# Eight-core streaming encoder step: norm tiles turned by crossbar DMA instead of TensorE, two gate products per step, an earlier final norm

## The chip, the cores and the metric

The kernel runs on the 8 cores of one Trainium2 chip, the same program on each. A core has TensorE (PE) for matrix products and transposes, VectorE (DVE), ScalarE (ACT) and GpSimd (POOL) for the rest, SyncE (SP) for issuing DMAs, and 16 DMA engines. The metric is the device time of the slowest core in microseconds (us), the median of the runs.

## The reference

One layer of an encoder trunk over 4 x 8192 prompt tokens and 16 x 64 further tokens, width 1024. Cut to what matters here:

```python
h = _rmsnorm(x, norm1_g)
z = h @ w_in                                  # [pool a 512 | u 512 | v 512]
u, v = gelu(z[..., 512:1024]), gelu(z[..., 1024:])
pool_out = ((trailing_mean(a) - a) @ pool_w) * pool_scale
gmlp_out = u * (einsum('gij,bnjgd->bnigd', masked_ws, v) + gmlp_b)
x = x + concat([pool_out, gmlp_out]) @ w_out
f = _rmsnorm(x, norm2_g) @ w_up               # 1024 -> 4096
x = x + square(relu(f)) @ w_down              # 4096 -> 1024
y = _rmsnorm(x, normf_g)                      # the final norm
```

`_rmsnorm` scales each token (row) by the inverse root of its mean square and each column by `g`.

## The kernel before

Each core has 33 tiles of 128 tokens, in nine groups: group 0 has three tiles, group 1 two, groups 2 to 8 four each. x stays in `XS` (SBUF, nine slots of 128 tokens x 1024 channels, float32), weights come in blocks of 1 MB through the five slots of `RING`. TensorE contracts over the partition dimension, so a normalised tile (tokens on partitions) has to be turned: channels onto partitions, in eight 128-channel blocks.

A norm of tile n takes five parts. `N1_sq` or `N2_sq` (ACT, L316) sums the squares; `rs` (POOL, L323 and L324) makes the scale of two tiles; `N1_apply` or `N2_apply` (DVE, L330) writes the normalised bf16 tile into one of three `HB` buffers, in turn; `N1_T` or `N2_T` turns it: eight transposes on TensorE into a PSUM bank (L339) and a copy on ACT (L343) to `HT` for the first norm, `H2T` for the second. Both are one form of `norm_T`, with the tile's destination as an argument. `final_sq`, `final_rs` and `final_out` are the final norm; `final_out` also issues the store to `yall` from POOL's queue (L652), and `load_x` (L370) then loads a later group's tile into the slot that the store has left.

The order of each engine's work is written out by hand: a list `main` of steps for TensorE, and `side(k, ...)`, which hangs further work behind step k; `run` goes through both, and every helper appends to the queue of its engine (`add`). Engines run their own queues in order and wait on semaphores for what `reads` and `writes` name. A buffer that is still read makes its next writer wait.

The first two groups go through two passes together (`for c in range(2)`), which also make weight sums and differences in scratch memory; group 2's first half runs beside them. Then comes the loop over groups, `for i in range(2, NG)`: pass i does the MLP of group i and, as side work, the norms, input projection, mixers and output projection of group j = i + 1. Six passes, i = 2 to 7, have such a j; I count them from one ("the third pass" is i = 4). `main` of a pass has 60 steps: 32 up-projections `UP` (steps 0 to 31, L577; ACT's Relu, L582; VectorE's square, L584), then 28 down-projection parts `DN` (L624), seven products M of four steps each, in the order 3, 4, 5, 7, 2, 1, 6 (a fast form with seven in place of eight products). After the second half of a product VectorE adds its PSUM bank to x (L634); product 6 goes on in the bank of product 1, so step 56 needs the add behind step 54, and step 57 the one behind step 55.

The side work of group j by step: `load_x` at 6, `N1_sq` 17 to 20, `N1_apply` 21 to 24, `N1_T` 23 to 26, input projection `WI_au` 27 to 34 (L385, all of `HT` wanted) and `WI_v` 35 to 38 (L406), pool mixer `PL` 31 to 34, `gate` 39 to 42 (four small products, L475, then on VectorE an add, L482, and a product, L491), output projection `WO` 43 to 50 (L504; add to x, L509), `N2_sq` 48 to 51, `N2_apply` 53 to 56, `N2_T` 55 to 58. Step 0 of the next pass wants all of `H2T`. `UP` and `DN` use five PSUM banks in turn, all side work the other three (`next_front`).

Of the kernel before, what the change touches and what calls it, by code (L numbers as in the profile page):

```python
# [117 lines left out]
def build_nc():  # L118
# [35 lines left out]
    with contextlib.ExitStack() as es:  # L154
# [71 lines left out]
        def ht(i):  # L226
            return HT1 if i == 1 else HT[:, :, 16:528]
# [18 lines left out]
        def h2t(i):  # L246
            return H2T1 if i == 1 else H2T
# [11 lines left out]
        def schedule(P, order, record):  # L259
# [94 lines left out]
            def N1_T(i, n):  # L354
                hb = hbs[("1", i, n)]
                norm_T(HB[hb], [("HB", hb)], ht(i)[:, :, n * 128:(n + 1) * 128], ht_res(i, n))

            def N2_sq(i, n):
                sq("2", n, xap(i, n), [xres(i, n)])
# [403 lines left out]
            for c in range(2):  # L763
# [47 lines left out]
                else:  # L811
# [13 lines left out]
                    for n in range(4):  # L825
                        side(nup + 2 + n, L(N2_apply, 2, n))
                        side(nup + 4 + n, L(N2_T, 2, n))
                run(main, sides)

            for i in range(2, NG):  # L830
# [8 lines left out]
                            main.append(L(DN, i, M, c, n))  # L839
                prev = [(0, 0), (0, 1), (0, 2), (1, 0), (1, 1)] if i == 2 else [(i - 1, n) for n in range(4)]  # L840
                if i == 2:
                    side(0, *[L(final_sq, 0, n) for n in range(3)], L(final_rs, 0, 3))
                    side(2, *[L(final_out, 0, n) for n in range(3)])
                    side(3, *[L(final_sq, 1, n) for n in range(2)], L(final_rs, 0, 2))
                    side(5, *[L(final_out, 1, n) for n in range(2)])
                else:
                    side(0, L(final_sq, i - 1, 0), L(final_sq, i - 1, 1), L(final_rs, 0, 2))
                    side(1, L(final_sq, i - 1, 2), L(final_sq, i - 1, 3), L(final_rs, 2, 4))
                    for n in range(4):
                        side(2 + n // 2, L(final_out, i - 1, n))  # L850
# [6 lines left out]
                if j < NG:  # L857
                    for n in range(4):
                        side(6, L(load_x, j, n))
                        side(17 + n, L(N1_sq, j, n))  # L860
                        side(21 + n, L(N1_apply, j, n))
                        side(23 + n, L(N1_T, j, n))
                    side(18, L(rs, "1", 0, 2))
                    side(20, L(rs, "1", 2, 4))
                    for m in range(8):
                        side(27 + m, L(WI_au, j, m))
                    for n in range(4):
                        side(35 + n, L(WI_v, j, n))
                    side(31, L(PL_pre, j))
                    for g in range(4):  # L870
                        side(31 + g, L(PL, j, g))
                        side(39 + g, L(gate, j, g))
                    side(35, L(PL_post, j))
                    for hh in range(2):
                        for n in range(4):
                            side(43 + hh * 4 + n, L(WO, j, n, hh))
                    for n in range(4):
                        side(48 + n, L(N2_sq, j, n))
                        side(53 + n, L(N2_apply, j, n))
                        side(55 + n, L(N2_T, j, n))  # L880
                    side(49, L(rs, "2", 0, 2))
                    side(51, L(rs, "2", 2, 4))
                else:
                    side(55, L(final_sq, i, 0), L(final_sq, i, 1), L(final_rs, 0, 2))
                    side(56, L(final_out, i, 0, "sp"), L(final_out, i, 1, "sp"))
                    for n in (2, 3):
                        side(59, L(final_sq, i, n), L(final_rs, n, n + 1))
                    side(59, L(final_out, i, 2, "sp"), L(final_out, i, 3, "sp", 2))
# [77 lines left out]
```

How the kernel before makes its waits and increments, by code:

```python
        def run(engname, e, final=False):  # L77
            waited = {}
            pe_ch = prog.engchan["pe"]
            for fn, waits, chn in prog.ops[engname]:
                need = {}
                for w in waits:
                    if engname == "pe" and w.chan is pe_ch:
                        continue
                    if w.val > need.get(w.chan, 0):
                        need[w.chan] = w.val
                for ch, v in need.items():
                    if waited.get(ch, 0) >= v:
                        continue
                    e.wait_ge(ch.sem, v)
                    waited[ch] = v
                ins = fn(e)
                ins.then_inc(chn.sem, chn.inc)
            if final:
                for ev in final_waits:
                    e.wait_ge(ev.chan.sem, ev.val)
```

## Time and profile before

| | us |
|---|---|
| median of 3 runs (lowest, highest) | 1289.81 (1289.68, 1290.63) |
| the profiled execution | 1289.96 |
| its span on the slowest core (core 7) | 1288.2 |
| spans of the eight cores | 1284.0 to 1288.2 |
| TensorE busy | 1212.3 (94% of the span) |
| VectorE busy | 638.0 (50%) |
| ACT busy | 400.7 (31%) |
| DMA | 261.93 MB, mean 203 GB/s |
| transposes of norm tiles (L339) | 43.6 busy, 536 instructions |

The page gives busy time and shares for the whole span; the waits, the order of time and the DMAs come from queries of the trace, all of core 7. In the rows of the last section a timeline row has start, duration, engine, line, operation, what it writes and reads (`out<-in`), the shapes and the count of merged instructions; in brackets the idle time of its engine just before and what ended it. A waits row has the total, how often, and the longest. A DMA row has the count, the KB of each and the median time from issue to landing. A windows row has the busy time of PE, PEld (weight loads), DVE, ACT and POOL with the number of instructions, then TensorE's granted clock, the DMA engines' busy share and GB/s. Names such as `L339` are lines of the kernel; `ps` is PSUM.

### The profile page before, as it was taken

The numbers are of one execution on the slowest core, as the hardware profiler recorded it, in microseconds if no ns is written. First come the engines' busy times: TensorE is split into PE (matmuls) and PEld (weight loads), VectorE is DVE, ScalarE is ACT, GpSimd is POOL, SyncE is SP. The second block draws the span as 40 slices with busy tenths as digits, with TensorE's granted clock in tenths as the row PEclk, the third lists the DMA queues.
The fourth block names the chain that finished last, engine by engine and source line by source line (L and its number), as shares of the span: only waits on it lengthen the run. The fifth ranks groups of instructions, "written<-read, shape, count | busy, mean of one in ns | idle before, by whom it ended". The sixth has DMA issues, their size and how long they took to land.

```text
span 1288.2 us, 17796 instructions; the slowest of 8 cores (1284.0 to 1288.2 us)
## 1 busy us (share of the span) xinstructions
PE 1212.3 (94%) x6236; PEld 588.1 (46%) x6236; DVE 638.0 (50%) x1022; ACT 400.7 (31%) x678; POOL 100.8 (8%) x195
## 2 busy tenths in 40 slices
PE   5679998999799999999999999999999999999996
PEld 2336545543344444444444444444444444444442
DVE  2633636383355533665455534664455534764344
ACT  4324212314420255114520255114520355114301
POOL 4010000101000010001000010001000020001001
PEclk9879999999899999999999999999999999999998
DMA  9998866968634883457735783458634883758473
GB/s 179 187 228 227 183 198 203 163 225 280 196 120 174 262 270 122 163 198 279 243 119 175 261 283 114 173 193 282 230 131 164 270 278 110 186 200 281 175 262 145
DMA packets 44518, 261.93 MB, mean 203 GB/s; under 512 B 7360, under 2 KB 7488, under 8 KB 17552
## 3 DMA queue, kind: packets, MB, share of 16 engines
q1 hardware_dynamic: 31424, 206.84, 47.3%
q0 software_dynamic: 13008, 53.97, 18.3%
q8 instruction: 51, 0.84, 0.3%
q14 instruction: 35, 0.29, 0.1%
HBM read 240.22 MB, written 42.82 MB: 220 GB/s over the span
## 4 chain that ended last, share of the span: by engine, by line
PE 83%; DMA 6%; DVE 5%; issue 3%; ACT 1%; POOL 1%; DVEq 0%; POOLq 0%; SPq 0%; ACTq 0%
PE ps L577 25%; PE ps L624 25%; PE ps L504 9%; PE ps L385 8%; PE ps L538 5%; PE ps L552 5%; PE ps L406 4%; DMA XS<-xall 3%; PE ps L339 2%; DMA yall<-XS 2%; DVE HB L330 1%; DMA WSMT<-gmlp_ws 1%; DVE ps L482 1%; DVE XS L649 1%; ACT JUNK L316 1%
## 5 line engine op out<-in xcount | busy, mean ns | idle before, releaser
L577 PE MATMUL ps<-H2T,RING 128*128 128x512 bf16 x1792 | 399.3, 381 | 2.7 <-DMA RING<-scr_up 2.7
L577 PEld LDWEIGHTS ps<-H2T,RING 128*128 128x128 bf16 x1792 | 175.1, 98 | 210.9 <-issue 7.2
L624 PE MATMUL ps<-RING,ST 128*128 128x512 bf16 x1120 | 258.9, 379 | 0.0
L584 DVE TENSOR_TENSOR ST<-ST 128x512 bf16<-128x512 bf16 x224 | 93.8, 424 | 284.6 <-ACT ST L582 283.7
L582 ACT ACTIVATE ST<-ps 128x512 bf16<-128x512 f32 x224 | 132.2, 595 | 212.1 <-PE ps L577 210.4
L316 ACT ACTIVATE JUNK<-XS 128x1024 bf16<-128x1024 f32 x100 | 105.5, 1055 | 288.5 <-DVE XS L509 218.7
L634 DVE TENSOR_TENSOR XS<-XS,ps 128x512 f32<-128x512 f32 x140 | 96.1, 686 | 142.4 <-PE ps L624 138.0
L624 PEld LDWEIGHTS ps<-RING,ST 128*128 128x128 bf16 x1120 | 108.6, 98 | 126.5
L385 PE MATMUL ps<-HT,WAU 128*128 128x512 bf16 (+2 forms) x512 | 119.3, 379 | 0.6 <-ACT HT L343 0.6
L624 PE MATMUL ps<-RING,SB 128*128 128x512 bf16 x448 | 104.9, 379 | 0.0
L509 DVE TENSOR_TENSOR XS<-ps,XS 128x512 f32<-128x512 f32 x66 | 45.5, 689 | 68.4 <-PE ps L504 67.3
L385 PEld LDWEIGHTS ps<-HT,WAU 128*128 128x128 bf16 x512 | 50.9, 100 | 59.6 <-issue 3.6
L339 PE MATMUL ps<-IDB,HB 128*128 128x128 bf16 (+1 forms) x536 | 43.6, 228 | 36.1 <-DVE HB L330 35.1
L552 PE MATMUL ps<-RING,ST 128*128 128x512 bf16 x320 | 71.5, 379 | 0.0
L504 PE MATMUL ps<-RING,MIXP 128*128 128x512 bf16 x224 | 57.5, 379 | 8.1 <-DVE HT L491 8.1
L624 PEld LDWEIGHTS ps<-RING,SB 128*128 128x128 bf16 x448 | 42.8, 98 | 47.2
L406 PE MATMUL ps<-WV,HT 128*128 128x512 bf16 x248 | 59.6, 386 | 2.7 <-DMA WV<-w_v 2.7
L323 POOL TENSOR_SCALAR SS<-SS 128x2 f32<-128x2 f32 (+3 forms) x34 | 8.6, 253 | 671.4 <-ACT JUNK L316 671.2
L339 PEld LDWEIGHTS ps<-IDB,HB 128*128 128x128 bf16 (+1 forms) x536 | 36.6, 102 | 52.8 <-issue 41.6
L343 ACT ACTIVATE H2T<-ps 128x1024 bf16<-128x1024 bf16 x31 | 31.8, 1024 | 82.7 <-PE ps L339 82.7
L504 PE MATMUL ps<-RING,HT 128*128 128x512 bf16 x224 | 57.5, 379 | 0.0
L596 DVE TENSOR_TENSOR ST<-ST 128x1024 bf16<-128x1024 bf16 x84 | 54.9, 684 | 0.0
(84 smaller groups left out, 925.8 us busy)
## 6 DMA issues: line engine op xcount, KB each, us to landing
RING<-scr_dn SPq DMA_DIRECT2D x98, 1024.0 KB, 5.3
RING<-scr_up SPq DMA_DIRECT2D x56, 1024.0 KB, 7.6
RING<-w_mlp POOLq DMA_DIRECT2D x16, 1024.0 KB, 12.1
XS<-xall POOLq DMA_DIRECT2D x30, 512.0 KB, 16.3
yall<-XS POOLq DMA_DIRECT2D x29, 512.0 KB, 6.7
RING<-scr_wo SPq DMA_DIRECT2D x14, 1024.0 KB, 5.1
scr_dn<-RING SPq DMA_DIRECT2D x10, 1024.0 KB, 7.6
scr_up<-RING SPq DMA_DIRECT2D x8, 1024.0 KB, 9.5
```

What stands on the lines that cost most here:

```text
L316: add("act", lambda e: e.activation(out=JUNK[0:np_], in_=ap, func=AF.Square, scale=1.0 / 32, accum_out=SS[kind][0:np_, j:j + 1]), reads=re ...
L339: i_ = e.transpose(out=bankbf(fb)[:, k * 128:k * 128 + np_], in_=src[0:np_, k * 128:(k + 1) * 128], identity=IDB[0:np_, 0:np_])
L385: i_ = e.matmul(bank(fb)[:, 0:h0 + T], lhsT=WAU[:, m, k, :], rhs=rhs, start=(k == 0), stop=(k == 7))
L406: i_ = e.matmul(bank(fb)[:, :], lhsT=H[:, k, n * 128:(n + 1) * 128], rhs=WV[:, k, :], start=(k == 0), stop=(k == 7))
L504: i_ = e.matmul(bank(fb)[:, :], lhsT=mix(i, k, n * 128, (n + 1) * 128), rhs=W[:, k, :], start=(k == 0), stop=(k == 7))
L538: i_ = e.matmul(bank(ub)[:, 0:T], lhsT=RING[s][:, k, mm_ * 128:(mm_ + 1) * 128], rhs=HX[:, k, 0:T], start=(k == 0), stop=(k == 7))
L552: i_ = e.matmul(bank(ub)[:, :], lhsT=HID[h](j0 + kk, n * 128, (n + 1) * 128), rhs=RING[s][:, kk, :], start=(kk == 0), stop=(kk == 7))
L577: i_ = e.matmul(bank(ub)[:, :], lhsT=RING[s][:, k, (m % 4) * 128:(m % 4 + 1) * 128], rhs=H2T[:, k, :], start=(k == 0), stop=(k == 7))
L582: add("act", lambda e: e.activation(out=ST[:, m, :], in_=bank(ub)[:, :], func=AF.Relu), writes=[("BANK", ub)] + rr)
L584: add("dve", lambda e: e.tensor_tensor(out=ST[:, m, :], in0=ST[:, m, :], in1=ST[:, m, :], op=ALU.mult), writes=rr)
L624: i_ = e.matmul(bank(ub)[:, :], lhsT=lh(kk), rhs=RING[s][:, kk, :], start=(c == 0 and kk == 0 and M not in CONT), stop=(c == 1 and kk == 7 ...
L634: add("dve", lambda e, x=x, op_=op_: e.tensor_tensor(out=x, in0=x, in1=bank(ub)[:, :], op=op_), writes=[("BANK", ub), xres(i, rb * 2 + n)])
```

## The change

For groups 3 to 8, `N1_T` and `N2_T` are replaced by `N1_D` and `N2_D`: one DMA, issued by ACT, that reads the `HB` tile and writes it turned to `HT` or `H2T`. Groups 0 to 2 keep the transposes on TensorE. The squares and normalisations of both norms come earlier by some steps, the turned tiles too. The four gate products hang two by two behind steps 39 and 40. Group 0's final norm moves from the loop's first pass into the pass before it, and group 1's moves up behind steps 0 and 2. In the diff the new helpers come first, then the second pass of the first two groups (c = 1), the loop's first pass (i = 2), and the side work of group j.

```diff
+            def turn(src, res, dst, dst_res, nm):
+                add("act", lambda e: e.dma_start_transpose(out=dst, in_=src), reads=res, writes=dst_res, dma=nm)
+
+            def N1_D(i, n):
+                hb = hbs[("1", i, n)]
+                turn(HB[hb][:], [("HB", hb)], ht(i)[:, :, n * 128:(n + 1) * 128], ht_res(i, n), f"xb1_{n}")
+
+            def N2_D(i, n):
+                hb = hbs[("2", i, n)]
+                turn(HB[hb][:], [("HB", hb)], h2t(i)[:, :, n * 128:(n + 1) * 128], h2_res(i, n), f"xb2_{n}")
...
+                    for n in range(3):
+                        side(nup + 16 + n, L(final_sq, 0, n))
+                    side(nup + 18, L(final_rs, 0, 3))
+                    for n in range(3):
+                        side(nup + 19, L(final_out, 0, n))
...
-                    side(0, *[L(final_sq, 0, n) for n in range(3)], L(final_rs, 0, 3))
-                    side(2, *[L(final_out, 0, n) for n in range(3)])
-                    side(3, *[L(final_sq, 1, n) for n in range(2)], L(final_rs, 0, 2))
-                    side(5, *[L(final_out, 1, n) for n in range(2)])
+                    side(0, *[L(final_sq, 1, n) for n in range(2)], L(final_rs, 0, 2))
+                    side(2, *[L(final_out, 1, n) for n in range(2)])
...
-                        side(17 + n, L(N1_sq, j, n))
-                        side(21 + n, L(N1_apply, j, n))
-                        side(23 + n, L(N1_T, j, n))
-                    side(18, L(rs, "1", 0, 2))
-                    side(20, L(rs, "1", 2, 4))
+                        side(15 + n, L(N1_sq, j, n))
+                        side(18 + n, L(N1_apply, j, n))
+                        side(20 + n, L(N1_D, j, n))
+                    side(16, L(rs, "1", 0, 2))
+                    side(18, L(rs, "1", 2, 4))
...
-                        side(39 + g, L(gate, j, g))
+                        side(39 + g // 2, L(gate, j, g))
...
-                        side(48 + n, L(N2_sq, j, n))
-                        side(53 + n, L(N2_apply, j, n))
-                        side(55 + n, L(N2_T, j, n))
-                    side(49, L(rs, "2", 0, 2))
-                    side(51, L(rs, "2", 2, 4))
+                        side(47 + n, L(N2_sq, j, n))
+                        side(50 + n // 2, L(N2_apply, j, n))
+                        side(51 + n, L(N2_D, j, n))
+                    side(48, L(rs, "2", 0, 2))
+                    side(50, L(rs, "2", 2, 4))
```

The changed kernel has eleven lines more ahead of the loops, so its line numbers are higher by 11 from L366 on (L624 becomes L635, L475 becomes L486).

TensorE's queue around the gates, before (L624 is a step, L475 a gate product, L504 the output projection):

```order
L624 MATMUL ps<-RING,ST 128x512 x8
L475 MATMUL ps<-WSMT,V 128x128 x4
L624 MATMUL ps<-RING,SB 128x512 x8
L475 MATMUL ps<-WSMT,V 128x128 x4
L624 MATMUL ps<-RING,SB 128x512 x8
L475 MATMUL ps<-WSMT,V 128x128 x4
L624 MATMUL ps<-RING,SB 128x512 x8
L475 MATMUL ps<-WSMT,V 128x128 x4
L624 MATMUL ps<-RING,SB 128x512 x8
L504 MATMUL ps<-RING,MIXP 128x512 x4
```

The same place in the changed kernel (L635, L486, L515):

```order
L635 MATMUL ps<-RING,ST 128x512 x8
L486 MATMUL ps<-WSMT,V 128x128 x8
L635 MATMUL ps<-RING,SB 128x512 x8
L486 MATMUL ps<-WSMT,V 128x128 x8
L635 MATMUL ps<-RING,SB 128x512 x24
L515 MATMUL ps<-RING,MIXP 128x512 x4
```

Two gate products stand together now, and three steps lie between the last of them and the output projection in place of one.

VectorE's queue at the second norm, before, with the numbers of the `HB` buffers (L634 adds a down-projection bank to x, L509 the output projection, L330 normalises):

```order
L509 TENSOR_TENSOR XS<-ps,XS 128x512
L634 TENSOR_TENSOR XS<-XS,ps 128x512 x2
L330 SCALAR_TENSOR_TENSOR HB1<-XS,RS2,G2B 128x1024
L634 TENSOR_TENSOR XS<-XS,ps 128x512
L330 SCALAR_TENSOR_TENSOR HB2<-XS,RS2,G2B 128x1024
L634 TENSOR_TENSOR XS<-XS,ps 128x512
L330 SCALAR_TENSOR_TENSOR HB0<-XS,RS2,G2B 128x1024
L330 SCALAR_TENSOR_TENSOR HB1<-XS,RS2,G2B 128x1024
L634 TENSOR_TENSOR XS<-XS,ps 128x512 x2
```

The same place in the changed kernel (L645, L520):

```order
L520 TENSOR_TENSOR XS<-ps,XS 128x512
L330 SCALAR_TENSOR_TENSOR HB1<-XS,RS2,G2B 128x1024
L330 SCALAR_TENSOR_TENSOR HB2<-XS,RS2,G2B 128x1024
L645 TENSOR_TENSOR XS<-XS,ps 128x512 x2
L330 SCALAR_TENSOR_TENSOR HB0<-XS,RS2,G2B 128x1024
L330 SCALAR_TENSOR_TENSOR HB1<-XS,RS2,G2B 128x1024
L645 TENSOR_TENSOR XS<-XS,ps 128x512 x4
```

All four normalisations stand ahead of the last four adds now, and the fourth writes the buffer (`HB1`) that the first turn reads.

ACT's queue there, before (L397 and L411 take the input projection out of PSUM, L316 is a square, L582 the next pass's first Relu):

```order
L582 ACTIVATE ST<-ps 128x512
L397 ACTIVATE UT<-ps 128x512 x4
L411 ACTIVATE V<-ps 128x512 x4
L316 ACTIVATE JUNK,SS<-XS 128x1024 x4
L343 ACTIVATE H2T<-ps 128x8x128 x4
L582 ACTIVATE ST<-ps 128x512
```

And in the changed kernel (L593, L408, L422):

```order
L593 ACTIVATE ST<-ps 128x512
L408 ACTIVATE UT<-ps 128x512 x4
L422 ACTIVATE V<-ps 128x512 x4
L316 ACTIVATE JUNK,SS<-XS 128x1024 x4
L359 DMA_TRANSPOSE H2T<-HB 128x8x128 x4
L593 ACTIVATE ST<-ps 128x512
```

Where ACT copied four turned tiles out of PSUM it now issues four DMAs that turn them, all of them behind the fourth square. In the first norm each of the four stands behind one Relu, as the copies did.

## Rows read from the trace of the kernel before

**Rows 1.** The page, parts 1 and 4: busy time (share), instructions; chain's shares.
```profile
PE 1212.3 (94%) x6236; PEld 588.1 (46%) x6236; DVE 638.0 (50%) x1022; ACT 400.7 (31%) x678; POOL 100.8 (8%) x195
...
PE 83%; DMA 6%; DVE 5%; issue 3%; ACT 1%; POOL 1%; DVEq 0%; POOLq 0%; SPq 0%; ACTq 0%
```

**Rows 2.** Waits of TensorE (us, times, longest): whole span, then 300 to 1171.
```profile
PE ps L339 <- DVE HB L330: 35.1, 15, 13.6
...
PE ps L339 <- DVE HB L330: 9.3, 3, 7.4
PE ps L504 <- DVE HT L491: 8.1, 6, 1.6
PE ps L577 <- DMA RING<-scr_up: 2.7, 1, 2.7
```

**Rows 3.** Timeline of TensorE, third pass: start, us, instruction [idle before].
```profile
595.04 41.60 PE L577 MATMUL ps<-H2T,RING 128*128 128x512 bf16 x192
...
730.41 0.61 PE L339 MATMUL ps<-IDB,HB 128*128 128x128 bf16 x8
730.86 1.89 PE L624 MATMUL ps<-RING,ST 128*128 128x512 bf16 x8
...
739.10 21.10 PE L577 MATMUL ps<-H2T,RING 128*128 128x512 bf16 x97
```

**Rows 4.** Timeline around the fourth gate product, third pass: VectorE, TensorE.
```profile
694.93 0.69 DVE L491 TENSOR_TENSOR HT<-ps,UT 128x512 bf16<-128x512 f32 x1
...
695.88 1.02 PE L504 MATMUL ps<-RING,MIXP 128*128 128x512 bf16 x4 [1.30 <-DVE HT L491]
```

**Rows 5.** Timeline of ACT and VectorE at that pass's second norm.
```profile
722.89 1.06 ACT L316 ACTIVATE JUNK<-XS 128x1024 bf16<-128x1024 f32 x1 [2.25 <-DVE XS L509]
...
725.17 1.28 DVE L330 SCALAR_TENSOR_TENSOR HB<-XS,RS,G2B 128x1024 bf16<-128x1024 f32 x1
```

**Rows 6.** Timeline of the loop's first pass: TensorE, ACT, POOL.
```profile
307.60 29.47 PE L577 MATMUL ps<-H2T,RING 128*128 128x512 bf16 x128 [2.72 <-DMA RING<-scr_up]
344.52 1.01 PE L339 MATMUL ps<-IDB,HB 128*128 128x128 bf16 x8 [7.45 <-DVE HB L330]
...
341.02 1.06 ACT L316 ACTIVATE JUNK<-XS 128x1024 bf16<-128x1024 f32 x1 [2.83 <-DMA XS<-xall]
...
300.56 0.62 POOL L652 DMA_DIRECT2D yall<-XS  x1 [2.12 <-DVE XS L649]
...
324.61 0.53 POOL L370 DMA_DIRECT2D XS<-xall  x1 [2.05 <-DMA yall<-XS]
```

**Rows 7.** Third pass: POOL's last x load; DMA issues (median us to landing).
```profile
616.79 0.53 POOL L370 DMA_DIRECT2D XS<-xall  x1 [4.55 <-DMA yall<-XS]
...
XS<-xall POOLq DMA_DIRECT2D x4, 512.0 KB, 14.4
```

**Rows 8.** DMA issues in 1265-1288, 1090-1105, 629-646, 718-740; SP's timeline.
```profile
yall<-XS SPq DMA_DIRECT2D x2, 256.0 KB, 2.2
...
RING<-scr_dn SPq DMA_DIRECT2D x2, 1024.0 KB, 10.4
...
spp<-A SPq DMA_DIRECT2D x1, 30.0 KB, 10.7
...
RING<-scr_dn SPq DMA_DIRECT2D x3, 1024.0 KB, 4.8
...
RING<-scr_up SPq DMA_DIRECT2D x5, 1024.0 KB, 7.8
RING<-scr_dn SPq DMA_DIRECT2D x1, 1024.0 KB, 6.2
...
722.03 0.32 SPq L296 DMA_DIRECT2D RING<-scr_dn  x1
```

**Rows 9.** Windows: engines' busy us (instructions), granted clock, DMA share, GB/s.
```profile
629.00:646.00 17.00, 17.00 (x104) 8.68 (x103) 9.73 (x15) 11.82 (x19) 1.87 (x4) 1.00 0.39 145
...
724.00:739.00 15.00, 15.00 (x95) 7.80 (x94) 7.90 (x9) 4.14 (x5) 0.93 (x2) 1.00 0.96 310
```

## The prediction

> **What bounds the kernel now.** I read the busy shares first, then who waited for whom on TensorE, then single passes in order of time, then the DMAs. TensorE is busy 94% of the span and the chain that ended last runs through it for 83% [rows 1]. It waits 35.1 us for normalised rows before their transposes, but only 9.3 of that in the loop over groups, beside 8.1 for the gate and 2.7 for a weight block [rows 2]; the other 25.8 us lie ahead of the loop, where the change leaves the norms as they are. Of the 9.3, 7.4 fall in the loop's first pass [rows 6], the rest, 1.9, in two later ones. In a pass of that loop TensorE has no gap but 1.3 us ahead of the output projection [rows 4]: what leaves its queue there comes off the time, as long as nothing new is late. One step of such a pass, eight products, is 41.60 / 24 = 1.73 us, and one pass is 144.1 us, 595.04 to 739.10 [rows 3]; the granted clock there is 1.00, the 2.4 GHz level [rows 9], and fewer gaps give it no cause to fall. The profiled execution took 1289.96 us, 1.8 over its span and 0.15 over the median, so I count from 1289.96.
>
> **Transposes (removed).** A turn of one norm tile, eight 128x128 transposes, moves the next product from 730.41 to 730.86 [rows 3]: 0.45 us of TensorE's queue, not the 0.61 its row shows, since ends overlap. Six passes hold eight turns each, 48 in all: 48 x 0.445 = **-21.4 us**. ACT loses 48 copies out of PSUM; it is 31% busy [rows 1], so that is worth nothing by itself.
>
> **Gates (moved).** The four gate products stood behind steps 39 to 42; the last is multiplied by VectorE at 694.93 to 695.62, and the projection starts at 695.88 after 1.30 us of waiting [rows 4]. Two per step starts the last product two steps (3.5 us) earlier, and VectorE has nothing between the eight gate operations now: the wait goes, six times, 8.1 us [rows 2]. The fourth product takes the PSUM bank of the first and so waits for its two VectorE operations, 1.4 us after it was made, against one step of 1.73 us, with one add ahead of them in VectorE's queue; I put 0.15 us on each pass. Sum **-7.2 us**.
>
> **First group's final norm (moved).** In the first pass the last x tile of the next group is asked for at 324.61, behind an output store, its square starts at 341.02 after waiting for it, and TensorE stands 7.45 us until 344.52 [rows 6]. The change sends the first group's stores out in the pass before, by its place about 7 us ahead of 300.56 [rows 6], the second group's with them, and the loads behind both on POOL's queue. With the square also two steps earlier, the last tile is then ready about when step 27 wants it. Counting the 1.9 us of later passes, -9.3 us, of which I give 1 back. The other side: the three early stores, 1.5 MB, meet the up-projection loads that already cost 2.72 us at 307.60 [rows 6], in a stretch where DMA is not idle. Between nothing (the wait even goes, -2.7) and 8 us I take +3, since 512 KB at the 310 GB/s of a busy stretch [rows 9] is 1.7 us. Sum **-5.3 us**.
>
> **Crossbar turns (added).** No row shows one, so its time L from issue on ACT's queue to landing has to be bounded. Low end: a plain 256 KB store in the quiet end of the program lands in 2.2 us. High end: 30 KB in 512 small pieces took 10.7 us [rows 8]. Where does L begin to cost?
> Second norm: ACT's fourth square ends near 724.0 [rows 5], and all four turns stand behind it. There are three HB buffers, so the fourth normalisation on VectorE waits for the first turn to land: 724.0 + L, plus 1.28 [rows 5]. Behind it in VectorE's queue stands the add that empties the bank of step 54, 0.69 us like the gate's operation, and step 56, at 730.41 [rows 3], accumulates into that bank: TensorE waits once L is over 4.4 us. The fourth turn lands at 725.3 + 2L; the next pass's first product, due 737.3 without the transposes (730.41 plus four steps of 1.73), waits once L is over 6.0.
> First norm: the last x tile is asked for at 616.79 and lands 14.4 us later [rows 7], 631.2; the square, two more Relus, and ACT reaches the first turn near 633.6. The fourth normalisation waits for it here too, so the fourth turn lands at 634.9 + 2L, and the input projection of step 27 wants it at 595.04 + 28 x 1.73 = 643.5: TensorE waits once L is over 4.3. This stretch is quiet, DMA 0.39 busy; the second norm's is not, 0.96 [rows 9].
> I take 4 us in the quiet stretch and 5 in the busy one: nearest is the 256 KB transfer, the same bytes, at 2.2; weight loads of 1 MB go from 4.8 to 7.8 us between the two stretches [rows 8], which makes it 3.6 in the busy one, and the rest is a surcharge for small pieces. So the first norm costs nothing and the second 0.6 us. The turns also lengthen the weight loads beside them: the block asked for at 722.03 lands after 6.2 us at 728.2 [rows 8], 2.2 us before step 56 wants it; I put another 0.6 us there. 6 x 1.2 = **+7 us**, between 0 and, at L = 7.8 throughout, 6 x (7.0 + 3.6) = 64.
> The Trainium skill, page "DMA: Bandwidth & Descriptors", section "Latency and other measured facts", gives DMA transposes 261 GB/s; the 256 KB of a turn would then move in 1.0 us (an estimate from that page), L would stay below both limits, and the sum would be 1256. No run here shows it yet.
>
> **Sum.** 1289.96 - 21.4 - 7.2 - 5.3 + 7 = **1263 us**. With every turn and load hidden it is 1289.96 - 21.4 - 8.1 - 9.3 - 2.7 = 1248.
>
> **Rivals.**
> (a) Slower: the crossbar works in small pieces, and a turn takes the 10.7 us of the small-piece row. Then the first norm's fourth turn is 634.9 + 21.4 - 643.5 = 12.8 us late and the second's 725.3 + 21.4 - 737.3 = 9.4 us: 22.2 us in each of six passes, 133 us against a gain of 34, near 1389. It decides from L = 6.6 on, where 4L - 20.6 eats the 5.65 us that a pass gains. For it: the small-piece transfers also stretched the 1 MB load beside them to 10.4 us [rows 8]. Against it: those pieces are 60 bytes and go to HBM. The Trainium skill, page "VectorE: DVE Perf Modes", section "The three transpose paths", speaks for it: 1309 ns for a 128x128 block by DMA against 390 ns on TensorE. Eight blocks one after the other would be 10.5 us (an estimate from that page), much as in (a), near 1384; its TensorE figure does not hold here, where a block costs 0.445 / 8 = 56 ns of queue.
> (b) L lies between: 6.6 to 7.8 us, 1291 to 1320.
> (c) The turns land in time, but the weights don't. From step 52 on TensorE uses up 1 MB per two steps, 3.45 us, and DMA already moves 310 GB/s at 0.96 share [rows 9]. Four turns bring 1 MB more, read and written: 3.4 to 6.8 us of transfer. The block of step 56 has 2.2 us in hand, the first up block, asked for one step (1.73 us) after that one and 7.8 us under way, is there at 731.6 and wanted at 737.3: 5.7 us. So 1 to 4.6 us come back as TensorE waits for RING; at 2.7 a pass it is 1279.
> (d) The change doesn't do what it says: the transposes' time is not free. Against it stands that the four steps with a turn each take 739.10 - 730.41 = 8.69 us, 2.17 apiece, where others take 1.73 [rows 3]. Only a chance balance of gain and wait would give 1290.
>
> **How the numbers follow.** The forecast (1248 to 1271) has 0.50, (c) 0.17, no change 0.04, (b) 0.11, (a) 0.18. A measurement of this kernel can tell about 0.2%, 2.6 us, from no change. Faster is the forecast and (c): 0.67; slower is (a) and (b): 0.29. The range reaches from everything hidden, 1248, to the upper end of (b), 1320, and holds 0.82; the likeliest case's own range is 1248 to 1271.
>
> **What would show it.** Right: 384 fewer transposes on TensorE; passes some 140.5 us apart instead of 144.1; no wait ahead of the output projection; ACT's turns landing in 3 to 5 us. Steps wrong one by one: a wait of the up-projection for H2T, or of the input projection for HT, says L is over its limit; a wait of the down-projection for XS's adds says VectorE stood at its fourth normalisation; waits for RING say (c); a wait longer than 2.72 us near 300 us says the early stores cost more than they bring. The prediction fails as a whole if L is over 6.6 us.

## The result, and the profile after

The changed kernel took **1486.5 us** (median of 4 runs, 1472.53 to 1501.62); the kernel before took 1289.87 beside it (4 runs). The ratio is 1.1431, 95% interval 1.1407 to 1.1456: 14% slower. The prediction said 1263, with a range of 1248 to 1320. It was wrong in size and in sign. Medians here and below are of all runs of a kernel and ratios of its undisturbed runs alone (here 1472.53 and 1476.37), so the two can differ; for first_norm_only and second_norm_only, which have no ratio, the profiled run is taken.

The profiled execution took 1472.53 us, its span on core 6 is 1471.0; the spans of the other cores reach from 1402.3 to 1470.1. First the page, parts 1 and 4, which answer to [rows 1]: busy time (share) and instructions, then the chain that ended last, by engine and by line.

```profile
PE 1214.8 (83%) x5747; PEld 571.5 (39%) x5852; DVE 636.2 (43%) x1022; ACT 354.2 (24%) x630; POOL 108.5 (7%) x195
...
PE 65%; DMA 18%; ACTq 8%; DVE 3%; issue 3%; ACT 2%; POOL 1%; DVEq 0%; SPq 0%; POOLq 0%
PE ps L588 23%; PE ps L635 15%; DMA H2T<-HB 10%; ACTq L359 8%; PE ps L515 8%; PE ps L396 7%; PE ps L549 4%; PE ps L417 4%; DMA HT<-HB 4%; PE ps L563 3%; DMA XS<-xall 2%; DMA scr_dn<-RING 2%; DVE HB L330 1%; ACT JUNK L316 1%; DMA RING<-scr_up 1%
```

TensorE went from 94% to 83% busy. 22% of the chain (10 + 8 + 4) is now the turns: two tiles of DMA and ACT's queue while it issues them (L359). The waits of TensorE over the whole span answer to [rows 2] (us, times, longest; L588 is the up-projection, L635 the down-projection, L645 its add to x, L396 the input projection):

```profile
PE ps L588 <- DMA H2T<-HB: 123.3, 6, 27.6
PE ps L635 <- DVE XS L645: 51.8, 6, 13.0
PE ps L339 <- DVE HB L330: 24.2, 12, 13.3
PE ps L396 <- DMA HT<-HB: 11.0, 5, 7.3
PE ps L588 <- DMA RING<-scr_up: 5.5, 1, 5.5
```

Three waits are new: 123.3 for the second norm's turned tiles, 51.8 for the adds behind VectorE's fourth normalisation, 11.0 for the first norm's tiles. The gate's 8.1 us is gone. The DMA issues of the whole span (count, KB, median us from issue to landing) show the price of a turn:

```profile
RING<-scr_up SPq DMA_DIRECT2D x56, 1024.0 KB, 11.4
...
HT<-HB ACTq DMA_TRANSPOSE x24, 4.4
H2T<-HB ACTq DMA_TRANSPOSE x24, 27.3
```

A first-norm turn lands in 4.4 us, a second-norm turn in 27.3. Core 6 is the slowest core; on the other seven the medians are 4.6 to 6.8 and 19.6 to 23.6. The up blocks take 11.4, where the same row of the kernel before has 7.6:

```profile
RING<-scr_up SPq DMA_DIRECT2D x56, 1024.0 KB, 7.6
```

**One second norm in order of time.** In the loop's second pass on core 6, the timelines of SP, ACT, VectorE and TensorE read:

```profile
614.08 66.34 SPq L296 DMA_DIRECT2D RING<-scr_up  x8
...
614.39 30.85 ACTq L359 DMA_TRANSPOSE H2T<-HB  x4
...
627.83 1.28 DVE L330 SCALAR_TENSOR_TENSOR HB<-XS,RS,G2B 128x1024 bf16<-128x1024 f32 x1 [9.78 <-DMA H2T<-HB]
629.03 1.28 DVE L645 TENSOR_TENSOR XS<-XS,ps 128x512 f32<-128x512 f32 x2
...
629.97 9.05 PE L635 MATMUL ps<-RING,ST 128*128 128x512 bf16 x31 [9.06 <-DVE XS L645]
657.03 50.61 PE L588 MATMUL ps<-H2T,RING 128*128 128x512 bf16 x220 [18.01 <-DMA H2T<-HB]
```

SP begins to send the next pass's up blocks at 614.08 and ACT the turns at 614.39. ACT needs 30.85 us only to issue the four. The first turn has landed when VectorE's fourth normalisation starts, 627.83: 13.4 us after its issue began. The other three, asked for one by one, landed 30.8, 28.9 and 22.4 us after their issue. The add runs at 629.03, TensorE has stood 9.06 us for it, and later stands 18.01 us for the fourth turn. Windows of the same stretch (length; busy time and instructions of PE, PEld, DVE, ACT, POOL; granted clock, DMA share, GB/s) show what the waits left behind:

```profile
596.00:614.00 18.00, 17.95 (x84) 8.15 (x84) 11.92 (x19) 4.23 (x7) 0.93 (x2) 1.00 0.64 222
614.00:630.00 16.00, 6.88 (x32) 2.98 (x32) 6.11 (x8) 0.37 (x2) 1.73 (x2) 0.81 1.44 184
630.00:633.00 3.00, 3.00 (x8) 1.05 (x9) 0.30 (x1) 0.00 (x0) 0.00 (x0) 0.50 0.30 75
630.00:657.00 27.00, 8.97 (x31) 3.45 (x32) 1.68 (x3) 0.00 (x0) 0.00 (x0) 0.69 0.90 152
657.00:660.00 3.00, 2.97 (x8) 1.07 (x9) 0.00 (x0) 0.00 (x0) 0.00 (x0) 0.50 0.16 68
657.00:675.00 18.00, 17.92 (x73) 7.79 (x75) 7.83 (x12) 8.88 (x17) 5.52 (x11) 0.88 0.45 161
```

Before the turns 84 products took 17.95 us at clock 1.00 (2.4 GHz), 0.214 each. The first 3 us behind TensorE's 9 and 18 us of standing have a granted clock of 0.50, the 1.2 GHz level. From 630 to 657, the 18 us of standing included, it averages 0.69, from 657 to 675 it averages 0.88, and 31 products take 8.97 (0.289 each), 73 take 17.92 (0.245 each). That is 31 x 0.075 + 73 x 0.032 = 4.7 us more in this pass.

The DMA engines look full from 630 to 657, share 0.90, yet move 152 GB/s. The queues in 612 to 660 (packets, MB, share of 16 engines; q10 is ACT's queue with the turns, q1 SP's) and the issues:

```profile
q10 hardware_dynamic: 4224, 1.05, 54.0%
q1 hardware_dynamic: 864, 6.29, 46.8%
...
RING<-scr_up SPq DMA_DIRECT2D x5, 1024.0 KB, 21.3
...
H2T<-HB ACTq DMA_TRANSPOSE x4, 25.6
```

Four turns are 4224 packets, 1056 apiece, of 1.05 MB / 4224 = 250 bytes. Their times add up to 0.54 x 48 x 16 = 415 us, 98 ns a packet. A share over 1, as the 1.44 from 614 to 630, means that times of packets overlap, so this is how long a packet was under way, waiting included, and not how long it kept an engine from others. The five up blocks beside them land in 21.3 us.

**Where the time went.** The span grew by 1471.0 - 1288.2 = 182.8 us. The new waits are 123.3 + 51.8 + 11.0 = 186.1; the waits for RING grew by 5.5 - 2.7 = 2.8. The gains: 21.4 of transposes, 8.1 at the gate, 35.1 - 24.2 = 10.9 for normalised rows. Together +148.5. Of the 34 us left, the slower clock after the waits makes up most if the pass above is typical: 6 x 4.7 = 28.

### The profile page after: what moved, and what is told of

It is laid out like the page before. It is cut to its first block, busy times and chain, and to the rows that moved or that the text cites. A ratio compares the mean times of both kernels' runs of the same rounds, so it can differ in the third digit from the quotient of the medians.

```text
span 1471.0 us, 17011 instructions; the slowest of 8 cores (1402.3 to 1471.0 us)
## 1 busy us (share of the span) xinstructions
PE 1214.8 (83%) x5747; PEld 571.5 (39%) x5852; DVE 636.2 (43%) x1022; ACT 354.2 (24%) x630; POOL 108.5 (7%) x195
## 3 DMA queue, kind: packets, MB, share of 16 engines
q10 hardware_dynamic: 50688, 12.59, 13.4%
## 4 chain that ended last, share of the span: by engine, by line
PE 65%; DMA 18%; ACTq 8%; DVE 3%; issue 3%; ACT 2%; POOL 1%; DVEq 0%; SPq 0%; POOLq 0%
PE ps L588 23%; PE ps L635 15%; DMA H2T<-HB 10%; ACTq L359 8%; PE ps L515 8%; PE ps L396 7%; PE ps L549 4%; PE ps L417 4%; DMA HT<-HB 4%; PE ps L563 3%; DMA XS<-xall 2%; DMA scr_dn<-RING 2%; DVE HB L330 1%; ACT JUNK L316 1%; DMA RING<-scr_up 1%
## 5 line engine op out<-in xcount | busy, mean ns | idle before, releaser
L588 PE MATMUL ps<-H2T,RING 128*128 128x512 bf16 x1756 | 407.6, 391 | 130.9 <-DMA H2T<-HB 123.3
L588 PEld LDWEIGHTS ps<-H2T,RING 128*128 128x128 bf16 x1792 | 179.0, 100 | 355.7 <-issue 156.3
L635 PE MATMUL ps<-RING,ST 128*128 128x512 bf16 x1099 | 267.5, 393 | 52.9 <-DVE XS L645 51.8
L593 ACT ACTIVATE ST<-ps 128x512 bf16<-128x512 f32 x224 | 132.8, 596 | 502.2 <-PE ps L588 480.7
L635 PEld LDWEIGHTS ps<-RING,ST 128*128 128x128 bf16 x1120 | 112.2, 101 | 195.3 <-issue 71.9
L316 ACT ACTIVATE JUNK<-XS 128x1024 bf16<-128x1024 f32 x100 | 105.3, 1053 | 286.0 <-DVE XS L520 212.2
L645 DVE TENSOR_TENSOR XS<-XS,ps 128x512 f32<-128x512 f32 x140 | 95.4, 686 | 141.5 <-PE ps L635 136.8
L396 PE MATMUL ps<-HT,WAU 128*128 128x512 bf16 (+2 forms) x505 | 119.8, 382 | 12.1 <-DMA HT<-HB 11.0
L635 PE MATMUL ps<-RING,SB 128*128 128x512 bf16 x432 | 101.2, 379 | 0.8
L396 PEld LDWEIGHTS ps<-HT,WAU 128*128 128x128 bf16 x512 | 50.6, 100 | 72.8 <-issue 18.8
L520 DVE TENSOR_TENSOR XS<-ps,XS 128x512 f32<-128x512 f32 x66 | 45.5, 689 | 66.7 <-PE ps L515 65.6
L563 PE MATMUL ps<-RING,ST 128*128 128x512 bf16 x312 | 70.8, 379 | 0.4
L330 DVE SCALAR_TENSOR_TENSOR HB<-XS,RS,G2B 128x1024 bf16<-128x1024 f32 x33 | 41.6, 1279 | 56.4 <-DMA H2T<-HB 56.1
L323 POOL TENSOR_SCALAR SS<-SS 128x2 f32<-128x2 f32 (+3 forms) x34 | 15.5, 455 | 683.7 <-ACT JUNK L316 683.5
L635 PEld LDWEIGHTS ps<-RING,SB 128*128 128x128 bf16 x448 | 43.4, 98 | 50.0
L515 PE MATMUL ps<-RING,MIXP 128*128 128x512 bf16 x220 | 56.9, 379 | 1.5 <-DVE ST L555 1.3
L515 PE MATMUL ps<-RING,HT 128*128 128x512 bf16 x222 | 57.2, 379 | 0.1
L549 PE MATMUL ps<-H2T,RING 128*128 128x384 bf16 x256 | 48.5, 338 | 1.4 <-ACT H2T L343 1.4
L330 DVE SCALAR_TENSOR_TENSOR HB<-XS,RS,G1B 128x1024 bf16<-128x1024 f32 x33 | 42.0, 1280 | 16.0 <-DMA G1B<-norm_g 7.6
## 6 DMA issues: line engine op xcount, KB each, us to landing
RING<-scr_up SPq DMA_DIRECT2D x56, 1024.0 KB, 11.4
RING<-w_mlp POOLq DMA_DIRECT2D x16, 1024.0 KB, 12.8
```

The lines of the kernel that those rows point to most:

```text
L316: add("act", lambda e: e.activation(out=JUNK[0:np_], in_=ap, func=AF.Square, scale=1.0 / 32, accum_out=SS[kind][0:np_, j:j + 1]), reads=re ...
L330: add("dve", lambda e: e.scalar_tensor_tensor(out=HB[hb][:], in0=xap(i, n), scalar=RS[kind][:, n:n + 1], in1=gb[:], op0=ALU.mult, op1=ALU. ...
L396: i_ = e.matmul(bank(fb)[:, 0:h0 + T], lhsT=WAU[:, m, k, :], rhs=rhs, start=(k == 0), stop=(k == 7))
L515: i_ = e.matmul(bank(fb)[:, :], lhsT=mix(i, k, n * 128, (n + 1) * 128), rhs=W[:, k, :], start=(k == 0), stop=(k == 7))
L549: i_ = e.matmul(bank(ub)[:, 0:T], lhsT=RING[s][:, k, mm_ * 128:(mm_ + 1) * 128], rhs=HX[:, k, 0:T], start=(k == 0), stop=(k == 7))
L563: i_ = e.matmul(bank(ub)[:, :], lhsT=HID[h](j0 + kk, n * 128, (n + 1) * 128), rhs=RING[s][:, kk, :], start=(kk == 0), stop=(kk == 7))
```

## The experiments

In the expectations, A is the theory that the weight blocks beside the turns make them slow, C a rival that needs no such neighbours. In the later runs P looks for the cause in small pieces that share the DMA engines with the blocks, X in the turning itself, F in an early final norm that brings nothing. The recorded texts say what each expects. Ratios are to the kernel before on the same chip. Line numbers shift a little between kernels.

**no_turns.** Both norms go back to TensorE at their old steps; gates and early final norm stay.

```diff
-                        side(20 + n, L(N1_D, j, n))
+                        side(23 + n, L(N1_T, j, n))
...
-                        side(51 + n, L(N2_D, j, n))
+                        side(55 + n, L(N2_T, j, n))
```

> The changed kernel with both norms of groups 3 to 8 turned on TensorE again, at the steps of the kernel before; gates and the earlier final norm stay. Theory A (the crossbar turns are the whole loss, the two other parts gain what the prediction gave them, 7 and 5 us): 1270 to 1280 us, no TensorE wait ahead of the output projection, the 7.4 us wait of the loop's first pass gone. Theory B (a part of the loss comes from the moved gates or the early stores): over 1290 us.

Measured: 1283.35 against 1295.11, ratio 0.9914 (0.9895 to 0.9933), which is 11.1 us (8.6 to 13.5) of 1289.96. Without the turns, and the earlier steps that come with them, the change is a gain, so they alone make the loss. TensorE's waits from 300 to 1171:

```profile
PE ps L588 <- DMA RING<-scr_up: 6.0, 1, 6.0
PE ps L339 <- DVE HB L330: 5.2, 2, 4.2
```

The gate's 8.1 us is gone. The wait for normalised rows fell from 9.3 [rows 2] to 5.2, the one for an up block rose from 2.7 to 6.0.

**gates_only.** The two-by-two gates alone, everything else as before.

```diff
-                        side(39 + g, L(gate, j, g))
+                        side(39 + g // 2, L(gate, j, g))
```

> The kernel before with one part of the change alone: the four gate products two by two. Both norms are turned on TensorE at their old steps, and the first group's final norm stands at its old place. Theory A (each term of the prediction apart from the turns holds): the waits of the output projection for VectorE, 8.1 us in six passes, go, and 0.9 us of gate products waiting for a PSUM bank come in, so 0.9944 of the time before, 1282.6 on the chip of the profile of before. Theory F (the early final norm brings nothing, and the whole gain of 0.86% of the run without turns is the gates'): 0.991.

Measured: ratio 0.9943 (0.993 to 0.9955) in 5 rounds, 7.4 us (5.8 to 9.0). This is theory A's number, 0.9944, and F's 0.991 lies outside the interval; the gates are settled. What no_turns gained beyond that, 11.1 - 7.4 = 3.7 us, is left for the early final norm, with some 3 us of uncertainty.

**second_norm_only and first_norm_only.** One norm by DMA, the other on TensorE; the rest as in the changed kernel.

```diff
-                        side(20 + n, L(N1_D, j, n))
+                        side(23 + n, L(N1_T, j, n))
```

> The changed kernel with only the second norm of groups 3 to 8 turned by DMA; the first norm is turned on TensorE at the steps of the kernel before. Theory A: 1460 to 1500 us, the turns landing in 10 to 35 us as in the changed kernel. Theory B: about half the loss, near 1385 us.

Measured: the profiled run took 1463.45 against 1295.11, 13% slower; a second run took 1485.48. One norm carries all but a little of the loss, as A said. The turns landed in 27.0 us, as A had it too. TensorE's waits, whole span:

```profile
PE ps L588 <- DMA H2T<-HB: 94.0, 6, 23.1
PE ps L635 <- DVE XS L645: 71.4, 6, 15.6
```

The other kernel undoes the second norm's turns in the same way.

> The changed kernel with only the first norm of groups 3 to 8 turned by DMA; the second norm is turned on TensorE at the steps of the kernel before. Theory A (the loss is the second norm's turns, which run beside the next pass's weight loads): 1265 to 1280 us, the turns landing in 3 to 8 us, about 11 us of TensorE waits for HT. Theory B (crossbar traffic slows the kernel wherever it runs): well over 1300 us, landing times of 10 us and more here too.

Measured: the profiled run took 1313.24 against 1295.11, 1.4% slower; A had said a gain and some 11 us of waits, which was a miss. The wait and the turns' landing time:

```profile
PE ps L396 <- DMA HT<-HB: 31.0, 6, 7.3
...
HT<-HB ACTq DMA_TRANSPOSE x24, 5.9
```

At 5.9 us the turns are past the limit of 4.3 that the prediction worked out, and TensorE waits 31.0 / 6 = 5.2 us a pass. On the eight cores the turns' medians are 5.5 to 6.5, much as in the changed kernel (4.4 to 6.8). That the first norm's stretch isn't quiet for the whole of its turns is tested by first_norm_hold below.

**hold_weights.** The next pass's first up blocks are sent only after the second norm's turns have landed.

```diff
+                if key[0] == "up" and key[1] < 2 and key[-1] >= 3 and at not in st.setdefault("freed", set()):
+                    st.setdefault("held", []).append(at)
+                    return
...
+                    held = [("H2T", n) for n in range(4)] if (src[0] == "up" and src[1] < 4 and key[-1] >= 3) else []
...
+                if n == 3:
+                    for at in st.pop("held", []):
+                        st.setdefault("freed", set()).add(at)
+                        ring_load(at)
```

> The changed kernel, but the first up-projection weight blocks of the next pass are loaded only when the second norm's four turns have landed, so that only one or two down-projection blocks run beside them. Theory A (the turns are slow because their 256-byte packets share each DMA engine with 8 KB weight packets): the turns land in 3 to 8 us and TensorE waits under 10 us a pass for H2T, now partly for RING; 1300 to 1380 us. Theory C (four turns behind one another are slow by themselves, in ACT's queue or in the crossbar): landing times stay at 20 to 30 us and the weights come after them; 1480 us or more.

Measured: 1334.42, ratio 1.031 (1.0285 to 1.0335). TensorE's waits over the whole span, then the issues:

```profile
PE ps L404 <- DMA HT<-HB: 37.5, 6, 8.3
...
PE ps L596 <- DMA RING<-scr_up: 21.3, 8, 9.7
...
HT<-HB ACTq DMA_TRANSPOSE x24, 6.1
H2T<-HB ACTq DMA_TRANSPOSE x24, 3.3
```

This decides for A and against C: the same turns land in 3.3 us instead of 27.3 when no up blocks move beside them, and no row of TensorE's waits names a DMA to `H2T` any more. The price has moved: the held blocks come late (21.3 us for RING), and the first norm, untouched here, is over its limit (6.1 us, 37.5 of waits).

**plain_pieces and plain_rows.** The second norm's four DMAs stay where they are but copy instead of turning (the second norm's tile is left unturned): once in pieces of 256 bytes, once in rows of 2 KB.

```diff
-                turn(HB[hb][:], [("HB", hb)], h2t(i)[:, :, n * 128:(n + 1) * 128], h2_res(i, n), f"xb2_{n}")
+                add("act", lambda e: e.dma_start(out=h2t(i)[:, :, n * 128:(n + 1) * 128], in_=HB[hb][:].rearrange("p (k t) -> p k t", t=128)),
+                    reads=[("HB", hb)], writes=h2_res(i, n), dma=f"xb2_{n}")
...
+                add("act", lambda e: e.dma_start(out=H2T[:, 2 * n:2 * n + 2, :].rearrange("p k t -> p (k t)"), in_=HB[hb][:]),
```

> The changed kernel with the second norm's four DMAs as plain copies in place of turns: the same 256 KB from HB to H2T in pieces of 256 bytes, from ACT's queue with the same waits. The tile is not turned, so what the second half of the layer computes for groups 3 to 8 is left out of the comparison. Theory P (small packets beside 8 KB weight packets are what is slow): landing 10 to 30 us as with the turns, 1450 us or more. Theory X (the crossbar itself suffers from other traffic on the 16 engines, plain pieces don't): landing under 8 us, TensorE waiting under 3 us a pass for H2T, 1290 to 1320 us.

Measured: 1350.37 (quickest run 1347.16), ratio 1.0432 (1.041 to 1.0454). Waits of TensorE, then issues:

```profile
PE ps L636 <- DVE XS L646: 42.9, 6, 11.2
PE ps L397 <- DMA HT<-HB: 28.9, 6, 8.4
...
RING<-scr_up SPq DMA_DIRECT2D x56, 1024.0 KB, 7.9
H2T<-HB ACTq DMA_DIRECT2D x24, 256.0 KB, 12.2
```

> As the plain copy in 256-byte pieces, but each token's 2 KB goes to one place of H2T in one piece (not turned, so what the second half of the layer computes for groups 3 to 8 is left out of the comparison). Theory P: packets eight times as large, landing 3 to 6 us, 1290 to 1310 us. Theory X: the same. Together with the pieces it tells whether the bytes alone cost anything.

Measured: 1342.92 (1336.81 and 1349.03), ratio 1.0387 (1.033 to 1.0444).

```profile
PE ps L397 <- DMA HT<-HB: 35.6, 6, 8.6
PE ps L636 <- DVE XS L646: 25.9, 6, 5.5
...
H2T<-HB ACTq DMA_DIRECT2D x24, 256.0 KB, 8.2
```

So 256 KB beside the up blocks cost 8.2 us in long rows, 12.2 in 256-byte pieces, 27.3 turned. Neither P nor X has it alone: small pieces add 4 us, the turning another 15, and only the turning slows the blocks beside it (11.4 against 7.9). Only with the turning does TensorE wait for a DMA to `H2T`; neither copy leaves such a row. P had the landing of the pieces right and their time 100 us too high; for the rows both theories expected 3 to 6 us and at most 1310, a miss. Even the long rows miss the limit of 4.4 us for VectorE. A good part of what both copies lose is the first norm, which is still turned by DMA here (28.9 and 35.6).

**sp_queue.** All turns are issued by SP, in the queue of the up blocks.

```diff
-                add("act", lambda e: e.dma_start_transpose(out=dst, in_=src), reads=res, writes=dst_res, dma=nm)
+                add("sp", lambda e: e.dma_start_transpose(out=dst, in_=src), reads=res, writes=dst_res, dma=nm)
```

> The changed kernel with all turns issued from SP's queue, which also issues the weight loads, in place of ACT's. Theory P (a turn's packets take turns with the other queue's 8 KB packets): in one queue they only wait for what was issued before them, landing 3 to 10 us, no long wait for H2T, 1300 to 1390 us. Theory X: weight packets on the same engines still hold the crossbar up, landing 10 to 30 us, over 1430 us.

Measured: 1338.6, ratio 1.0353 (1.0332 to 1.0374).

```profile
PE ps L396 <- DMA HT<-HB: 30.6, 6, 7.1
PE ps L635 <- DVE XS L645: 29.9, 6, 5.7
...
H2T<-HB SPq DMA_TRANSPOSE x24, 7.7
```

In the blocks' own queue a turn of the second norm lands in 7.7 us, not 27.3. It is still over 4.4, and the adds still wait. The run changes two things at once, though: the turns share a queue with the blocks, and most blocks now stand behind them. SP's timeline in one pass:

```profile
584.56 7.43 SPq L359 DMA_TRANSPOSE H2T<-HB  x2
...
592.75 6.38 SPq L359 DMA_TRANSPOSE H2T<-HB  x2
599.28 26.91 SPq L296 DMA_DIRECT2D RING<-scr_up  x6
```

One up block stands between the turns and one just ahead of them, six behind. So that two queues are what makes a turn slow is not shown apart from the order; with hold_weights it says that the turns must not run beside many of the blocks.

**first_norm_hold.** The first norm alone by DMA, with the one or two weight blocks that would move beside its turns sent after them; the second norm on TensorE.

```diff
+                if st.get("turning"):
+                    st.setdefault("held", []).append(at)
+                    return
...
+                        reads=[("SCR", src)] + st.get("after", []), writes=[("RING", s)], dma=f"ring{s}")
...
+                if n == 3:
+                    st["turning"] = False
+                    st["after"] = [r for m in range(4) for r in ht_res(i, m)]
+                    for at in st.pop("held", []):
+                        ring_load(at)
+                    st["after"] = []
...
+                    side(18, N1_hold)
```

> Only the first norm of groups 3 to 8 is turned by DMA (the second on TensorE), and the one or two weight blocks that were loaded beside these turns, which have some 25 us in hand, are loaded after them. If the weight traffic is what slows the turns, they land in 3 to 4 us, the TensorE waits for HT (31 us with the weights beside them) fall under 8 us, and the kernel is 6 to 11 us faster than with both norms on TensorE, 20 us faster than before. If x loads from POOL's queue slow them as well, landing stays near 6 us and the time within 0.5% of before.

Measured: 1273.49 against 1292.71, ratio 0.9853 (0.9837 to 0.987). By its ratio it is ahead of the kernel before, the changed one and no_turns (0.9914). Waits from 300 to 1171, TensorE's timeline in the loop's first pass, the queue of the turns over the whole span, and their landing:

```profile
PE ps L600 <- DMA RING<-scr_up: 10.1, 2, 9.5
...
PE ps L408 <- DMA HT<-HB: 1.1, 1, 1.1
...
317.44 36.70 PE L600 MATMUL ps<-H2T,RING 128*128 128x512 bf16 x160 [9.47 <-DMA RING<-scr_up]
...
q10 hardware_dynamic: 25344, 6.29, 2.2%
...
HT<-HB ACTq DMA_TRANSPOSE x24, 2.8
```

With the weight blocks out of its way a turn lands in 2.8 us. Its packets took 0.022 x 16 x 1270.7 / 25344 = 18 ns each, under a fifth of the 98 above. One 9.47 us wait for an up block stands in the first pass, behind the early stores.

**hold_late_final.** first_norm_hold with the first group's final norm back at its old place (the second group's too, behind steps 3 and 5). The edit is shown against first_norm_hold.

```diff
-                    for n in range(3):
-                        side(nup + 16 + n, L(final_sq, 0, n))
-                    side(nup + 18, L(final_rs, 0, 3))
-                    for n in range(3):
-                        side(nup + 19, L(final_out, 0, n))
...
+                    side(0, *[L(final_sq, 0, n) for n in range(3)], L(final_rs, 0, 3))
+                    side(2, *[L(final_out, 0, n) for n in range(3)])
```

> The kernel first_norm_hold (first norm turned by DMA with the weight blocks beside the turns held back, second norm on TensorE) with the first group's final norm back at its old place in the loop's first pass. Theory A (the early final norm brings 5.3 us): slower than first_norm_hold by about 5 us, 0.989 of the time before. Theory F (it brings nothing: TensorE's wait for a normalised row in the loop's first pass, up to 7.4 us, was swapped for one of 9.5 us for an up block behind the early stores): 0.981 to 0.986; the 9.5 us wait for RING falls to about 2.7, and a wait of up to 7.4 us for HT takes its place.

Measured: 1272.94 against 1293.2, ratio 0.985 (0.9836 to 0.9864), no different from first_norm_hold. Waits from 300 to 1171 and the timeline of the first pass:

```profile
PE ps L600 <- DMA RING<-scr_up: 9.7, 2, 7.1
PE ps L408 <- DMA HT<-HB: 2.5, 1, 2.5
...
314.62 37.01 PE L600 MATMUL ps<-H2T,RING 128*128 128x512 bf16 x160 [7.14 <-DMA RING<-scr_up]
```

F's time came, its mechanism only in part: 9.5 us at one place became 7.1 plus 2.5 (for `HT`) at two. That gates_only, with late stores too, has 2.2 for an up block says little, since each profile shows its slowest core: from 285 to 380 the eight cores of gates_only wait 1.8 to 9.2 us there, those of hold_late_final 1.9 to 9.7 and those of first_norm_hold 3.2 to 11.8.

## Why the prediction was wrong

**The step that failed** is the size of L in the busy stretch, in the part on the crossbar turns. It took 5 us, from a plain 256 KB store of 2.2 us [rows 8], stretched as the weight blocks stretch. Measured: 27.3 in the median. Two things were wrong in that. The nearest row by bytes was not the nearest by kind: the row with 512 small pieces (10.7) was, and even that is two fifths of it. And the stretching was taken from the blocks of one queue: the very thing that was priced at 3.6 us there, a plain copy of 256 KB, took 8.2 when ACT's queue brought it beside the up blocks (plain_rows). The surcharge for small pieces, put at 1.4 us, was 4, and the turning itself, 15 more, had no term. The term's range ended at L = 7.8, so the small-piece row stood only as a rival, and what was measured lies outside both.

**The limits were right, and so were the places.** VectorE's fourth normalisation holding the add, the up-projection waiting for `H2T`, the input projection for `HT`: all three waits came where the text put them. The first one also in size: TensorE's wait should be L - 4.4, with the L of the first turn. In the pass shown L is 13.4, so 9.0; it waited 9.06. In the other five L is 17.4, 11.7, 10.2, 12.1 and 13.2, and TensorE waited 12.96, 7.33, 5.85, 7.73 and 8.87. By the medians, plain_pieces gives 12.2 - 4.4 = 7.8 and waited 42.9 / 6 = 7.2; plain_rows 3.8 and 4.3; sp_queue 3.3 and 5.0.

**Issue time was priced at nothing, and one L stood for all four turns.** For the fourth turn the text has ACT free as soon as VectorE is done. Here ACT was busy 30.85 us issuing the four, and the fourth left at 634.4, 5.3 us after its normalisation had ended (627.83 + 1.28 = 629.1). It landed 22.4 us later, 9 more than the first had needed. So the up-projection is 9.06 + 18.01 = 27.1 us late in this pass, where 2L - 12.0 would give 14.8 with the first turn's L.

**The first norm** was taken at 4 us, limit 4.3. It measured 4.4 in the changed kernel (11.0 us of waits, 7.3 of them in the loop's first pass) and 4.6 to 6.8 on its other cores, 5.9 in first_norm_only (31.0). The stretch was called quiet because a window of it showed a DMA share of 0.39 [rows 9], but first_norm_hold, where the blocks beside the turns are moved, lands in 2.8 and waits 1.1: the few blocks in it are enough.

**The clock** was not priced. The text said fewer gaps give it no cause to fall; with 186 us of new gaps the granted clock fell from 1.00 to 0.50 behind the two shown, some 28 us in all if other passes are like that one (an estimate).

**Rivals.** (a) had the sign and small pieces as its ground, and gave 1389; it fell short of the measured time although it put 12.8 us a pass on the first norm, where 11.0 / 6 = 1.8 were measured. For the second it had 9.4, against (123.3 + 51.8) / 6 = 29.2: L was over twice its 10.7, and its sum leaves out the issue time and the clock. (b) and (c) fell: L was nowhere near 7, and the blocks were not what TensorE waited for, though they did slow down. (d) fell: in first_norm_hold the transposes' time comes off once the turns are quick. Of the signs of a wrong step that the text listed, the waits for H2T, HT and XS showed, and so did a wait longer than 2.72 us near 300 us (5.5). Of the right ones two showed: 6236 - 5852 = 384 weight loads fewer on TensorE, and no wait ahead of the output projection.

**The other terms.** Gates: -7.2 predicted, -7.4 (5.8 to 9.0) measured; right. Final norm: -5.3 predicted, from +3 and -8.3. no_turns leaves 3.7 for it, hold_late_final next to nothing. The term that was mis-sized is the gain of 8.3. It was read off one core: from 285 to 380 the eight cores of the kernel before wait 0 to 7.4 us for normalised rows and 2.2 to 9.2 for an up block, and where one is long the other is short (7.5 to 10.4 together). In the mean of the cores the early stores took away 6.1 us of waiting for rows (gates_only against no_turns) and added 3.9 at the up blocks (4.3 to 8.2), 2.2 in all. With the squares two steps earlier as well, as the prediction wanted them, late stores leave 1.6 us of waiting for HT in hold_late_final, again in the mean of the cores, so there was little left to gain. Transposes: half of them, 24 x 0.445 = 10.7 us, went in first_norm_hold, which stands 0.9914 - 0.9853 = 0.6%, 7.9 us, ahead of no_turns. On the profiled cores it has 10.1 - 6.0 = 4.1 us more of waiting for RING, 1.1 more for HT and 5.2 less for normalised rows, which cancel. 10.7 and 7.9 agree within the some 3 us that the intervals leave.

**Three figures for a turn.** The Trainium skill, page "DMA: Bandwidth & Descriptors", section "Latency and other measured facts", has 261 GB/s for DMA transposes; 1.0 us a turn is an estimate from that page. The quickest landing here, with the weight blocks out of its way, is 2.8 us for 256 KB, so it doesn't hold for a turn of this size. The Trainium skill, page "Advanced Engine Details and Errata", section "X-Bar Transpose (TRN2)", says that transpose DMAs are as fast as regular ones. Beside the up blocks the runs say otherwise: 27.3 us against 12.2 for the same bytes in 256-byte copies. The Trainium skill, page "VectorE: DVE Perf Modes", section "The three transpose paths", has 1309 ns for a 128x128 block by DMA; with the weight blocks out of the way it is 2.8 / 8 = 0.35 us here, and beside the blocks 27.3 / 8 = 3.4.

**What stays open.** Why a turn's packets are under way for 98 ns beside plain 1 MB blocks of another queue, and for 18 without them, isn't shown. Plain pieces of nearly the same number and size took 12.2 us in the same place, so neither the count of packets nor two queues sharing the engines is all of it. Nor is it shown why the slowest core's turns (27.3) took longer than those of the others. Nor was it tried whether more `HB` buffers would free VectorE from the first turn.

## What to carry to other kernels

A transfer that replaces work on a busy engine is priced in the stretch where it will run, beside the transfers that run there, and by the row nearest in kind (piece size, queue, issue time), not in bytes. Work out the latest landing that each waiting engine allows first: here it was 4.3 and 4.4 us, and none of the second norm's transfers beside the up blocks met it (27.3 turned, 12.2 in pieces, 8.2 in rows, 7.7 from SP). Where such a transfer does pay, as in the first norm, it pays once the big loads beside it are sent after it: 0.9853 of the time before, against 1.014 for the same turns beside them.

## What the runs showed of the hardware

- A DMA turn of a 128x1024 bf16 tile is 1056 packets of some 250 bytes. With no weight loads beside it, it lands in 2.8 us; beside 1 MB loads from another queue in 27.3 on the slowest core, 19.6 to 23.6 on the others; from the queue of those loads, most of them behind it, in 7.7.
- With turns and plain loads together the DMA share says little of what moves: 0.90 and 152 GB/s, against 0.64 and 222 just before.
- Issuing can block the issuing engine: four turns held ACT's queue for 30.85 us, 1.25 for the first and 8.7 to 10.8 for each of the others. A timeline row of ACTq of that length is a sign of it.
- A wait of 9 to 18 us on TensorE costs more than itself: the granted clock was 0.50 in the first 3 us behind it, and products took 0.289 and 0.245 us in the mean instead of 0.214.
